# Last expert's latents finished in quadrant form, its context set first, context tile first among the outputs

## What is computed

```
def expert_choice_ffn(h, w_router, w_gate, w_up, w_down):      # per expert: cap = 2 n / 16 tokens
    gates, idx = lax.top_k(jnp.swapaxes(aff, 1, 2), cap)
    xe = jax.vmap(lambda hb, ib: hb[ib])(h, idx)
    a = jnp.einsum('becd,edf->becf', xe, w_gate)
    u = jnp.einsum('becd,edf->becf', xe, w_up)
    ye = jnp.einsum('becf,efd->becd', jax.nn.silu(a) * u, w_down) * gates[..., None]
    return jax.vmap(lambda yb, ib: jnp.zeros((n, d)).at[ib.reshape(-1)].add(yb.reshape(-1, d)))(ye, idx)

x = x + gate2 * expert_choice_ffn(h, *moe_w)
y_prompt = rms_norm(xp, g_final)       # context
y_sample = rms_norm(xs, g_final)       # latents
```

## Time and profile before

| | |
|---|---|
| time before, median of 3 runs | 1159.15 us (1158.74 to 1159.57) |
| time of the profiled execution | 1158.53 us |
| its span | 1156.7 us |
| busy: PE, DVE, ACT, POOL | 1096.4, 524.8, 369.2, 149.2 us |
| DMA | 302.14 MB, mean 261 GB/s |

### The profile page before, as it was taken

How to read it: one execution, slowest core, us unless ns; L and a number is a source line. 1 busy time by engine, 2 the same in 40 slices (tenths; PEclk the granted TensorE clock), 3 DMA queues, 4 the chain that set the end, 5 groups by cost and what they waited for, 6 DMA issues and landing times.

```text
span 1156.7 us, 28248 instructions
## 1 busy us (share of the span) xinstructions
PE 1096.4 (95%) x12557; PEld 817.2 (71%) x12557; DVE 524.8 (45%) x963; ACT 369.2 (32%) x860; POOL 149.2 (13%) x204
## 2 busy tenths in 40 slices
PE   6999999999999999999999999999999999999981
PEld 4679877777877777777867777777777777655650
DVE  3575458889958242334366133333322332223325
ACT  4333336777754122022163411112222222222012
POOL 2342450000000000002013111111011101100010
PEclk9999999999999999999999999999999999999996
DMA  9952232112051544359669999999999999999983
GB/s 358 302 222 73 74 73 67 35 24 47 1 216 54 182 146 142 105 190 300 239 252 412 410 406 405 408 406 407 405 410 413 406 407 407 405 410 409 409 301 110
DMA packets 87227, 302.14 MB, mean 261 GB/s; under 512 B 27217, under 2 KB 28498, under 8 KB 62018
## 3 DMA queue, kind: packets, MB, share of 16 engines
q1 hardware_dynamic: 80400, 276.00, 62.0%
q0 software_dynamic: 6288, 19.70, 6.0%
q10 hardware_dynamic: 418, 4.63, 1.0%
HBM read 276.46 MB, written 18.60 MB: 255 GB/s over the span
## 4 chain that ended last, share of the span: by engine, by line
PE 73%; DMA 11%; DVE 8%; issue 3%; ACT 2%; SPq 1%; POOLq 0%; ACTq 0%; POOL 0%; DVEq 0%
PE ps L1189 33%; PE ps L758 9%; PE ps L760 9%; PE ps L759 9%; DMA late<-in_w_exp_down_dram 5%; PE ps L984 2%; PE ps L968 2%; DVE neg_max L1777 2%; DMA x_dram<-y_row,rows_t 2%; PE ps L1007 1%; PE ps L1003 1%; DMA raw_first<-in_w_in_dram 1%; DMA x_f<-x_dram 1%; DVE q_lo_t L1769 1%; DMA raw<-in_w_in_dram 1%
## 5 line engine op out<-in xcount | busy, mean ns | idle before, releaser
L1189 PE MATMUL ps<-late,xe 128*32 128x256 f32 x3936 | 215.7, 379 | 0.0
L2090 DVE SCALAR_TENSOR_TENSOR y_row<-ps,gates,gate_q 32x256 f32<-32x256 f32 (+1 forms) x192 | 92.1, 480 | 255.3 <-PE ps L1189 252.6
L1189 PEld LDWEIGHTS ps<-late,xe 128*32 128x32 f32 x3936 | 150.4, 110 | 62.0
L1189 PE MATMUL ps<-late,ht 128*32 128x256 f32 x2400 | 134.6, 379 | 6.7 <-DMA late<-in_w_exp_down_dram 4.6
L1544 ACT ACTIVATE h_t<-ps 128x256 f32<-128x256 f32 x48 | 15.0, 385 | 382.9 <-PE ps L1189 382.9
L758 PE MATMUL ps<-w_hi,ht 128*128 128x512 f32 (+1 forms) x320 | 124.7, 390 | 0.0
L1189 PEld LDWEIGHTS ps<-late,ht 128*32 128x32 f32 x2400 | 89.4, 110 | 48.2 <-DMA late<-in_w_exp_down_dram 6.9
L760 PE MATMUL ps<-w_hi,ht 128*128 128x512 f32 (+1 forms) x320 | 121.8, 380 | 0.0
L759 PE MATMUL ps<-raw_lo,ht 128*128 128x512 f32 (+1 forms) x320 | 121.7, 380 | 0.0
L525 DVE TENSOR_TENSOR raw_lo<-raw,w_hi 128x1024 fp32r<-128x1024 f32 x48 | 57.7, 1225 | 79.1 <-ACT w_hi L520 78.5
L520 ACT ACTIVATE w_hi<-raw 128x1024 fp32r<-128x1024 f32 x48 | 48.8, 1052 | 122.8 <-DMA raw<-in_w_in_dram 67.9
(11 more groups left out here) (306 smaller groups left out, 1598.3 us busy)
## 6 DMA issues: line engine op xcount, KB each, us to landing
late<-in_w_exp_down_dram SPq DMA_DIRECT2D x50, 1024.0 KB, 28.8
late<-in_w_exp_up_dram SPq DMA_DIRECT2D x44, 1024.0 KB, 28.9
late<-in_w_exp_gate_dram SPq DMA_DIRECT2D x38, 1024.0 KB, 27.5
raw<-in_w_in_dram SPq DMA_DIRECT2D x16, 1024.0 KB, 5.5
raw<-in_w_exp_gate_dram SPq DMA_DIRECT2D x16, 1024.0 KB, 28.0
raw<-in_w_exp_up_dram SPq DMA_DIRECT2D x14, 1024.0 KB, 27.9
raw<-in_w_mod_dram SPq DMA_DIRECT2D x12, 1024.0 KB, 7.0
early<-in_w_exp_gate_dram SPq DMA_DIRECT2D x10, 1024.0 KB, 25.9
```

Source lines behind the costliest of these rows:

```text
L1189: mm = pe.matmul(out[32 * q:32 * q + 32, :], x[:, k, :], columns_of(w, q), start=(k == 0), stop=(k == KD - 1))
L2090: return dve.scalar_tensor_tensor(y_row[n % 2][32 * v:32 * v + count, 256 * q:256 * q + 256], bank(b, o, o + 256, src), gates[src, n % EG, ...
```

## The change

The rows of the last expert are split by set. Its **context** set is computed first in the down-projection (`sets_of`), and its 16 rows are added, squared, rooted and scaled by themselves, in token rows on partitions 64 to 79 of `x_l`. Its **latents** stay in quadrant form: x1_dram is seen as rows of 256 numbers, GpSimd gathers the latents' quarter rows into `x_lq` (128 x 256 for each set), VectorE multiplies and adds a whole set with one instruction each, ScalarE squares it, and a matmul with `quad_sum` (ones where two partitions belong to the same token) adds the four partial sums. The output goes back by quarter rows. For it GpSimd loads `g_final` once more, by quarters (`g_fin_q`, four transfers).

The tiles of x_f are loaded, finished and stored with the context tile first (`FINISH_ORDER`). The context's output scatter waits for the context tile's store alone (s_cout); the latents' two scatters wait for the four latent stores.

```
-            for t in range(NT):
+            for t in FINISH_ORDER:                                             # SyncE
                 sp.dma_start(x_f[:, t, :], x1_dram[t * P:(t + 1) * P, :]).then_inc(s_x[t], 16)
...
+            sp.wait_ge(s_fy, 1)
+            sp.dma_start(y_prompt[0], x_f[:, NTL, :]).then_inc(s_cout, 16)
+            for t in range(NTL):
+                sp.wait_ge(s_fy, t + 2)
+                sp.dma_start(ys[t], x_f[:, t, :]).then_inc(s_yout, 16)
...
+            for v in range(2):                                                 # TensorE
+                pe.wait_ge(s_lss, 3 + 2 * v)
+                pe.matmul(bank(3, v, v + 1), quad_sum[:, :, :].rearrange("p s a -> p (s a)"), ss_l[:, 2 + v:3 + v],
+                          start=True, stop=True).then_inc(s_vecturn, 1)
...
+            def latent_squares(v):                                             # ScalarE
+                act.wait_ge(s_last, 2 + v)
+                act.activation(sq_lq[:, :], x_lq[:, v, :], ACT.Square, accum_out=ss_l[:, 2 + v:3 + v]).then_inc(s_lss, 1)
+            def latent_rms(v):
+                act.wait_ge(s_vecturn, 3 + v)
+                act.activation(ss_l[:, 4 + v:5 + v], bank(3, v, v + 1), ACT.Sqrt, bias=eps, scale=1.0 / D).then_inc(s_lss, 1)
+            con = slice(CAPL, EROWS)
+            act.wait_ge(s_last, 1)
+            act.activation(sq_l[con, :], x_l[con, :], ACT.Square, accum_out=ss_l[con, 0:1]).then_inc(s_lss, 1)
+            act.wait_ge(s_lss, 1)
+            act.activation(ss_l[con, 1:2], ss_l[con, 0:1], ACT.Sqrt, bias=eps[con, :], scale=1.0 / D).then_inc(s_lss, 1)
+            finish_rms(0)
+            finish_rms(1)
+            latent_squares(0)
+            for i in range(2, NT):
+                finish_rms(i)
+            latent_rms(0)
+            latent_squares(1)
+            latent_rms(1)
...
+            activations(NE - 1)                                                # VectorE
+            context_added()
+            finish(0)
+            context_scaled()
+            finish(1)
+            latents_added(0)
+            for i in range(2, NT):
+                finish(i)
+            latents_added(1)
+            latents_scaled(0)
+            latents_scaled(1)
...
+            for q in range(4):                                                 # GpSimd, behind g_fin
+                pool.dma_start(g_fin_q[32 * q:32 * q + 32, :], g_final[256 * q:256 * q + 256].rearrange("(a n) -> a n", a=1)
+                               .to_broadcast([32, 256])).then_inc(s_gfin, 16)
```

More of the change, by code:

```diff
@@ L125 @@
 PART_BANKS = (0, 7)
+FINISH_ORDER = [NTL] + list(range(NTL))
 EXPERT_BLOCKS = [("g", 0), ("u", 0)]
@@ L703, in _ @@
             sp.wait_ge(s_scat, 16 * (NE - 1))
-            for t in range(NT):
+            for t in FINISH_ORDER:
                 sp.dma_start(x_f[:, t, :], x1_dram[t * P:(t + 1) * P, :]).then_inc(s_x[t], 16)
             ys = y_sample[0].rearrange("(t p) d -> t p d", p=P)
[L707 to L711, removed]
+            sp.wait_ge(s_fy, 1)
[3 more added lines that the diff above has]
+                sp.dma_start(ys[t], x_f[:, t, :]).then_inc(s_yout, 16)
+            sp.wait_ge(s_yout, 16 * NTL)
+            sp.wait_ge(s_lout, 48)
             sp.wait_ge(s_out, 32)
@@ L1227, in expert_block @@
                     last = n == NE - 1
-                    for at_set, v in enumerate((0, 2, 1)):
+                    for at_set, v in enumerate(sets_of(n)):
                         pe.wait_ge(s_ht2, SETS * n + at_set + 1)
@@ L2113, in _, with finish @@
             output(NE - 2)
[L2115 to L2119, removed]
+            def finish(i):
+                t = FINISH_ORDER[i]
+                dve.wait_ge(s_frs, i + 1)
+                if i == 0:
+                    dve.wait_ge(s_gfin, 80)
                 dve.reciprocal(rs[:, t:t + 1], rs[:, t:t + 1]).then_inc(s_dve, 1)
@@ L2138, in _, with context_added @@
[L2138 to L2149, removed]
+            def context_added():
+                dve.wait_ge(s_scat, 16 * (NE - 2))
+                dve.wait_ge(s_front, 1)
+                for q in range(4):
+                    output_piece(NE - 1, 2, q).then_inc(s_dve, 1)
+                dve.wait_ge(s_dve, own(4))
+                dve.wait_ge(s_xl2, 48)
+                dve.tensor_tensor(x_l[con, :], x_l[con, :], y_row[1][con, :], ALU.add).then_inc(s_last, 1)
@@ new lines, in context_scaled, with latents_added @@
+            def context_scaled():
+                dve.wait_ge(s_lss, 2)
+                dve.wait_ge(s_gfin, 80)
+                dve.reciprocal(ss_l[con, 1:2], ss_l[con, 1:2]).then_inc(s_dve, 1)
+                dve.wait_ge(s_dve, own())
+                dve.scalar_tensor_tensor(x_l[con, :], x_l[con, :], ss_l[con, 1:2], g_fin[con, :], ALU.mult, ALU.mult).then_inc(s_lrs, 1)
+            def latents_added(v):
+                dve.wait_ge(s_front, 2 + v)
+                dve.wait_ge(s_xl2, 48)
+                dve.scalar_tensor_tensor(y_lq[:, v, :], bank(v, 0, 256), gates[:, (NE - 1) % EG, v:v + 1], gate2_q[:, 0, :],
+                                         ALU.mult, ALU.mult).then_inc(s_dve, 1)
+                dve.wait_ge(s_dve, own())
+                dve.tensor_tensor(x_lq[:, v, :], x_lq[:, v, :], y_lq[:, v, :], ALU.add).then_inc(s_last, 1)
@@ new lines, in latents_scaled @@
+            def latents_scaled(v):
+                dve.wait_ge(s_lss, 4 + 2 * v)
+                dve.reciprocal(ss_l[:, 4 + v:5 + v], ss_l[:, 4 + v:5 + v]).then_inc(s_dve, 1)
+                dve.wait_ge(s_dve, own())
+                dve.scalar_tensor_tensor(x_lq[:, v, :], x_lq[:, v, :], ss_l[:, 4 + v:5 + v], g_fin_q[:, :], ALU.mult, ALU.mult)\
+                   .then_inc(s_lrs, 1)
+            con = slice(CAPL, EROWS)
+            dve.tensor_reduce(quad_sum[:, 0, :], ident.rearrange("p (s a) -> p a s", s=4), AX.X, ALU.add).then_inc(s_dve, 1)
```

68 lines of the change are left out of this document (33 added, 35 removed).

## The result

The changed kernel takes 1162.45 us (median of 8 runs, 1161.81 to 1163.8) where the kernel before takes 1159.27 (8 runs): the ratio is 1.0033, with a 95% interval of 1.0024 to 1.0042. The profiled execution has a span of 1160.7 us, 4.0 more than before. The ratios go by fast runs alone; the one slow run, of 6384 us in experiment 5, is not in them.

What follows compares the result with a forecast made beforehand. The prediction took a 30 us tail of short instructions waiting for one another as the bound. Its chain moved the end from 1151.0 to 1152.7, +1.7 us on 1159.15: about 1160.9 us, 8-in-10 range 1158.3 to 1163.4.

Steps and rivals of the forecast that it cites:

- The central step: In the tail, ScalarE waits for VectorE's context sum before any x_f tile; first tile's scaling 5.5 us later.
- Both stalls: ScalarE idle before the context's squares at 1129.63, then before the first latent half's squares at 1138.93, about 4 us.
- the sum: Forecast chain of start times through the tail, from weights at 1125.40 to the end at 1152.7 against 1151.0: +1.7 us.
- The last store as what releases the latent scatter: GpSimd's first latent scatter waits for the last x_f store landing at 1147.9, not VectorE, and starts 0.5 later, 1148.4.
- My 1.10 us: Delay of the last weights from four g_fin_q loads (0.39 us each) and two gathers (0.71 us together).
- my upper bound, 2.2: Largest delay of the last weights, if only half of the DMA engines take all six added transfers.
- the 0.055 us for each of the last 16 records: TensorE's time per matmul record after the last wait for weights, 7.98/144, used to date the first set.
- the 0.95 that I counted: From the last weights at 1125.40 to VectorE's first piece at 1126.35.
- 3.05 + 5.7: Last scatter's start to landing, 3.05 us, then landing to the end of the span, 5.7 us kept from before.
- The first, later weights: Rival: gathers or weights come later than reckoned, everything behind slides 1.6 to 5 us more, 1162.5 to 1166; chance 0.18.
- The faster case: Rival: last weights do not lag, first set ready 4.4 us sooner, -2.7 us, 1156.5; chance 0.07.
- The rule on small transfers: Rival: each of six added transfers holds the engines about a microsecond ahead of the last weights, 1166; chance 0.02.

Runs made afterwards that it cites:

- experiment 5: The kernel before with only the four g_fin_q loads and two quarter-row gathers added, their data unread: 1160.86 us, ratio 1.0014 to the kernel before.
- experiments 1 and 2: Changed kernel, ScalarE reordered. 1: two tiles before context's squares, latent halves behind all tiles, 1156.04 us. 2: first latent half kept ahead of third tile, 1158.33 us.
- experiment 7: The changed kernel without its two quad_sum matmuls, ScalarE taking roots from each partition's own partial sum: 1162.43 us, ratio 1.0031 to the kernel before.
- Experiment 4: The changed kernel with 6 and 9 identity matmuls before TensorE's last two waits for weights: 1161.55 us, ratio 1.0028 to the kernel before.
- experiment 8: The changed kernel with ScalarE taking tiles ahead of the sums and the six transfers issued behind the first set: 1155.16 us, ratio 0.9969 to the kernel before.
- 3 and 9: 3: changed kernel, six transfers behind first set, 1160.33 us. 9: that plus ScalarE's tiles first and VectorE's first latent half behind all tiles, 1154.38 us.

## Why the prediction was right, and where it was off

**The sign and the mechanism.** The central step held: ScalarE stands at VectorE's sums while the tiles lie in SBUF. Both stalls are in the trace, the second with 4.17 us where the sum had 3.9 (1134.83 + 0.20 to 1138.93), and experiments 1 and 2 give 6.3 us back by reordering ScalarE alone. The last store as what releases the latent scatter, the 0.5 us between them and the end by a scatter are as forecast; experiment 7 settled the release against the profile's own label.

**The size.** The span came out 2.3 us above my 1158.4. I had the kernels 1.7 us apart; the profiles are 4.0 apart, the ratio makes it 3.8 and the medians 3.2. The 1162.45 us lie in the range, but above 0.2%, where I had put a third of the chance and not the most. The 2.3 us of the span are made up so:

- *The weights, 0.63 us.* My 1.10 us were 1.73 (1.46 between the second profiles of the two kernels). I added up the engines' time that the six transfers hold, averaged over 16 engines. That time itself was right. Queue 0 from 1104 to 1126, in the kernel before and in the changed one:

```profile
q0 software_dynamic: 336, 1.18, 20.2%
q0 software_dynamic: 560, 1.57, 25.9%
```

That is 5.7% of 22 us, 1.25 us (1.06 between the second profiles). But only half of the engines still work while the last weights are awaited: the DMA share is 0.50 in the waits above, in both kernels, and the trace has eight packets in flight at a time there, where it has sixteen in the full stream before. So the end of the last weights is not the mean of 16 engines, and my upper bound, 2.2, was for the case of half of them. How much of the six transfers falls on the late half was not shown.
- *The clock, 0.86 us in this profile.* It is not in the sum at all. The step that failed is the 0.055 us for each of the last 16 records; they ran at half the clock after the longer wait. Experiment 4 shows that work in the wait keeps the clock up. What the clock costs in the time is not resolved: 0.3 to 0.6 us, within the error. What was argued and fell is that the length of the wait alone decides. All six profiles with an idle wait of 2.60 us or more have the fall (both of the changed kernel, experiments 1, 2, 5 and 7), four in the wait and two within 0.8 us after it. Of the five with 1.40 or 1.41 three do not have it (both of before, experiment 8) and two have it, within 0.2 us after the wait (3 and 9). What separates these is open.
- *The first piece, 0.26 us.* Even at full clock it takes 1.21 us from the end of the wait to the first piece, not the 0.95 that I counted.
- *The steps behind it, 0.4 us.* From the first piece to the start of the last scatter I had 1149.65 - 1126.35 = 23.3 us; the trace has 1151.82 - 1128.10 = 23.7. Over half of it is the context's scaling between the tiles: the scalings of the first tile, the context and the second tile start 1.51 us apart, not 1.39.
- *The close, 0.1 us.* From the start of the last scatter to the end of the span I had 3.05 + 5.7 = 8.75 us; the trace has 8.9. The two parts were both off, and that they cancel is luck. The scatter landed after 2.4 us instead of 3.05, and from the landing to the end it took 6.5 us instead of the 5.7 that I kept. The landing was the wrong mark: the span ends with GpSimd's drain. The drain ends 8.40 us after the last scatter's start in both profiles of before and 8.65 after it in all ten of the changed kernel and its forms, experiment 7 without the late matmuls among them. Experiment 5, which is the kernel before with nothing but the six transfers, has 8.74, so they lengthen the close by 0.3 us by themselves; why, no run shows.

**The change as such.** The prediction has VectorE's work as no shorter. That sum is wrong: it sets 6.0 us added against 5.9 removed, but the one scaling that goes away, its 1.48, is in neither; with it 4.4 us are added. The traces have 8.9 us of VectorE's work on the last expert before and 7.7 after, 1.2 less. No start in the forecast rests on that sum. Two costs of the change are shown: 6.3 us for ScalarE's order and 1.6 to 1.9 for the six transfers. With both undone and the rest kept (experiment 8) the kernel is 3.6 us faster than before. The rest as a whole is thus worth that much, and the changed kernel spent it and more; which part of it (the quarter rows, the context's early set, the order of the tiles) brings how much was not tested.

**The rivals.** The first, later weights, happened to a part of its size (0.6 us beyond the sum, where I had asked 3 to 5). The gathers were no cause: VectorE goes from the last piece to the sum at 1130.16 without a pause. The faster case needed weights 4 us sooner, and none of the profiles has them. The rule on small transfers, from the Trainium skill's page "DMA: Bandwidth & Descriptors" (section Bandwidth), would have added five microseconds by my estimate from its figure; the six transfers cost 1.6 to 1.9 in all, a third of that estimate, and nearer to the rows of bias_q.

## What to carry to other kernels

Before an engine's queue gets a wait for a partial result, ask what is already there behind it: here ready tiles stood behind a sum twice, and moving three calls on one engine was worth 6.3 us, more than all that the change costs net. Put small new loads behind the last big one that someone waits for; the mean over all engines was too low a price for them here. Read the end of the program from the engine whose drain ends last, not from the last landing. Where a wait of a few microseconds stands inside a matmul chain that something waits for, count it a second time, for the clock.

## What the runs showed of the hardware

- TensorE's granted clock went from 1.00 to 0.50 at an idle wait of 2.60 to 2.65 us in six profiles of six, in four of them inside the wait and in two 0.4 and 0.8 us after its end; in the changed kernel it came back at about 1132, 7 us later, while the engine worked. At a wait of 1.4 us it fell in two profiles of five. 128x128 identity matmuls, 0.25 to 0.31 us each, filled the waits in two kernels; in the one whose wait would have been 2.6 us this kept the clock up (one profile).
- Half of the DMA engines were unused (share 0.50 at about 205 GB/s, eight packets in flight) for most of the 1.4 to 2.6 us in which TensorE waited for the last weights, with more loads queued.
- The span ended 0.24 us after GpSimd's last DRAIN in all 13 profiles. The drain took 9.4 to 9.7 us, and its end came 8.40 us after the start of the last scatter before, 8.65 in the changed kernel and 8.74 in the kernel before with six more transfers.
- The profile can name the wrong releaser. The end of VectorE at 1150.42 was named, and the store that landed at 1150.0 was the cause; the closing wait was put down to TensorE, whose drain had ended 11 us before.
